# Latent tiles of a PEER layer: gathered expert rows replaced by an ordered walk over the expert table

## What is computed

```
qf = (xt @ w_q)                                # 8 heads x 2 parts of 128
s = einsum('thpd,hpnd->thpn', qf, sub_keys)    # scores of 128 keys per part
sv, si = top_k(s, 16)
cand = sv[:,:,0,:,None] + sv[:,:,1,None,:]     # 256 sums per head
top_s, pos = top_k(cand, 16)
idx = si[0]*128 + si[1] at pos                 # expert number
gate = softmax(top_s)
act = gelu(einsum('td,thkd->thk', x, u_tab[idx]))
out = einsum('thk,thkd->td', gate * act, v_tab[idx])
```

## Time and profile before

| | |
|---|---|
| time, median of 3 runs | 4426.65 us (4425.79 to 4427.81) |
| span of the profiled execution | 4415.7 us, first to last instruction |
| PE, DVE, ACT, POOL busy | 77%, 65%, 20%, 34% |
| PE weight loads busy | 35% |
| DMA | 1494.71 MB, 1344.36 MB of it gathered |
| last stage, from the first product of L777 | 1750 us to the end |

### The profile page before, as it was taken

How to read it: one execution, slowest core, us unless ns; L and a number is a source line. 1 busy time by engine, 2 the same in 40 slices (tenths; PEclk the granted TensorE clock), 3 DMA queues, 4 the chain that set the end, 5 groups by cost and what they waited for, 6 DMA issues and landing times.

```text
span 4415.7 us, 33544 instructions
## 1 busy us (share of the span) xinstructions
PE 3419.6 (77%) x7972; PEld 1528.7 (35%) x7972; DVE 2883.5 (65%) x6259; ACT 887.3 (20%) x2429; POOL 1498.4 (34%) x1297
## 2 busy tenths in 40 slices
PE   7767799976788886777787777777777677777777
PEld 1536344333443443233232333332333233333332
DVE  0535897847556877775775775774775774775774
ACT  0131321454322112111111111111111111111111
POOL 0000222212222223444454354344344444444343
PEclk9878899987898988889988899899899989898899
DMA  6324666756677788999999999999999999999997
GB/s 232 121 85 155 221 231 220 283 197 218 228 282 284 288 325 322 421 421 421 421 421 421 420 414 421 408 409 420 412 406 421 412 404 420 404 411 421 414 408 293
DMA packets 223619, 1494.71 MB, mean 338 GB/s; under 512 B 25388, under 2 KB 26668, under 8 KB 56660
## 3 DMA queue, kind: packets, MB, share of 16 engines
q0 software_dynamic: 184752, 1344.36, 75.7%
q1 hardware_dynamic: 37256, 143.43, 8.7%
q10 hardware_dynamic: 1440, 5.24, 0.3%
HBM read 1466.93 MB, written 26.02 MB: 338 GB/s over the span
## 4 chain that ended last, share of the span: by engine, by line
DMA 46%; PE 26%; DVE 10%; issue 9%; POOL 4%; ACT 3%; SPq 1%; POOLq 0%; DVEq 0%; ACTq 0%; PEldq 0%
DMA arena<-in_uv,idx 29%; DMA ring_e<-in_uv,idx 13%; PE wide L777 5%; PE bank L754 4%; PE bank L597 4%; PE bank L620 3%; PE wide L557 3%; POOL arena L516 3%; PE bank L737 3%; DMA arena<-in_w_q 2%; DVE ring_e L1253 2%; PE bank L568 1%; POOL ring_e L516 1%; PE bank L647 1%; DMA arena<-in_w_mod 1%
## 5 line engine op out<-in xcount | busy, mean ns | idle before, releaser
L777 PE MATMUL wide<-arena 128*128 128x512 f32 x3072 | 1521.6, 653 | 486.2 <-ACT arena L1032 464.0
L1564 DVE CUSTOM_DVE_ANT_0 arena<-arena,h2e 128x1024 f32<-128x1024 f32 x768 | 927.1, 1224 | 535.9 <-DMA arena<-in_uv,idx 511.8
L516 POOL DMA_INDIRECT arena<-in_uv,idx x768 | 900.7, 1173 | 1081.1 <-PE wide L777 918.9
L777 PEld LDWEIGHTS wide<-arena 128*128 128x128 f32 x3072 | 626.0, 209 | 1378.5 <-issue 767.7
L501 POOL DMA_INDIRECT ring_e<-in_uv,idx x256 | 306.0, 1195 | 1076.4 <-PE wide L557 516.3
L777 PE MATMUL wide<-ring_e,arena 128*128 128x512 f32 x1024 | 510.5, 656 | 162.3 <-ACT arena L1032 162.3
L1032 ACT ACTIVATE arena<-ident,small 128x128 f32<-128x128 f32 x1024 | 327.5, 390 | 623.2 <-DVE small L1571 609.5
L1564 DVE CUSTOM_DVE_ANT_0 ring_e<-ring_e,h2e 128x1024 f32<-128x1024 f32 x256 | 309.0, 1224 | 183.4 <-DMA ring_e<-in_uv,idx 183.0
L1253 DVE CUSTOM_DVE_ANT_0 ring_e<-ring_e,h2e 128x1024 f32<-128x1024 f32 x256 | 307.6, 1221 | 171.8 <-DMA ring_e<-in_uv,idx 171.2
L516 POOL DMA_INDIRECT ring_e<-in_uv,idx x256 | 287.0, 1121 | 375.5 <-PE wide L777 326.0
L777 PEld LDWEIGHTS wide<-ring_e,arena 128*128 128x128 f32 x1024 | 209.2, 210 | 463.4 <-issue 248.3
(11 more groups left out here) (180 smaller groups left out, 2413.6 us busy)
## 6 DMA issues: line engine op xcount, KB each, us to landing
arena<-in_w_mod SPq DMA_DIRECT2D x12, 2048.0 KB, 7.8
arena<-in_w_q SPq DMA_DIRECT2D x48, 512.0 KB, 10.4
arena<-in_w_cols SPq DMA_DIRECT2D x24, 512.0 KB, 3.9
arena<-in_uv,idx POOLq DMA_INDIRECT x768
arena<-in_x SPq DMA_DIRECT2D x20, 512.0 KB, 3.7
sc_d<-arena SPq DMA_DIRECT2D x36, 256.0 KB
arena<-in_w_vg SPq DMA_DIRECT2D x16, 512.0 KB, 4.2
arena<-in_w_out SPq DMA_DIRECT2D x16, 512.0 KB, 5.6
```

What stands on the lines that cost most here:

```text
L516: pool.indirect_dma_start(out=ring[k % RING], out_offset=None, in_=a["uv"], in_offset=bass.IndirectOffsetOnAxis(ap=idx[p][:, k:k + 1], axis=0)
L777: ins = pe.matmul(wide[p][:, c * 512:(c + 1) * 512], lhsT=diag[r], rhs=ring[r][:, D + c * 512:D + (c + 1) * 512], start=(first and r == 0) ...
L1564: dve.tensor_tensor_reduce(out=ring[r][:, 0:D], in0=ring[r][:, 0:D], in1=h2b[p], scale=1.0, scalar=0.0, op0=ALU.mult, op1=ALU.add, accum_o ...
```

## The change

Context tiles stay as they are. The latent tiles are taken in three passes of 2, 3 and 3 tiles, and each pass walks through all 128 blocks of 128 experts in order. A step of a pass: SP loads the block's u rows transposed (`in_ut`, a new input laid out by the host, 512 KB) and its v rows (512 KB); `scores_of` makes 8 products with the pass's tokens as columns (256 or 384); ACT takes the gelu from PSUM; `weigh` on DVE multiplies with the dense gates of that block; `sum_rows`, two steps later, adds v with 2 products of 512 columns for each tile.

The dense gates are made once per tile. `turn_choice` transposes the key numbers and gates; for each token DVE makes a one-hot row with the gate in it (`ones_for`), ACT one for the other key (Abs and then Relu over four tokens; of tile 3 DVE makes every second group), `spread` multiplies both into a 128x128 matrix per token, ACT copies four of them (`empty_spread`), SP stores 16 tokens at a time (1 MB, `store_group`) and loads them back for 8 expert blocks at a time (`load_gates`).

The query blocks of the latents become three, tiles 2 and 3, 4 to 6, 7 to 9 (`peer_blocks`), so w_q is loaded once more. Block 3 also holds tile 2's `spread` and tile 3's `pick_step`; tile 3's `spread` stands between it and the first step. Picks of tiles 4 to 7 stand in pass 0, of 8 and 9 in pass 1 (`PICKS`), and `spread` of a pass's tiles in the pass before. The final rows of the context tiles move into block 3; those of a pass stand in the first steps of the next.

```diff
+ETILES = 128
+PASSES = ((2, 2), (4, 3), (7, 3))
+LAG = 2
+UNIT = 4
+NG = 8
+def peer_blocks(s):
+    return [(0, 0, 2)] if s == 0 else [(1 + p, t, n) for p, (t, n) in enumerate(PASSES)]
@@ tensor, query blocks
+                    if b == 3:
+                        turn_choice(2)
                     for hp in range(HP + 1):
                         if hp < HP:
                             ... 8 products of the query
                         if hp:
                             ... scores of hp - 1
+                        if b == 3 and hp < HP:
+                            spread(2, 2 * hp)
+                            spread(2, 2 * hp + 1)
-            with pe.Fori(0, NT // 2 - 1) as i:
-                ... add_rows
+            for t, u in g_tiles[UNITS:2 * UNITS]:
+                if u == 0:
+                    turn_choice(t)
+                spread(t, u)
+            def scores_of(p, i):
+                n, slot = PASSES[p][1], nth[p, i] % URING
+                pe.wait_ge(*ut_in[slot].at((p, i)))
+                bk = claim(s_bank(p, i), S["s_empty"].at((p, i)))
+                for k in range(KD):
+                    ins = pe.matmul(bk[:, 0:n * P], lhsT=utb[slot][:, k * P:(k + 1) * P], rhs=H2T[1 + p][:, k, :], ...)
+            def sum_rows(p, i):
+                pe.wait_ge(*vt_in[slot].at((p, i)))
+                pe.wait_ge(*S["w_ready"].at((p, i)))
+                for j in range(n):
+                    for h, acc in enumerate(acc_banks(j)):
+                        ins = pe.matmul(acc, lhsT=w[:, j * P:(j + 1) * P], rhs=vtb[slot][:, h * 512:(h + 1) * 512], ...)
+            for n, (p, i) in enumerate(sweep):
+                scores_of(p, i)
+                if n >= LAG:
+                    sum_rows(*sweep[n - LAG])
+                for t in choice_in(p + 1, i):
+                    turn_choice(t, claim(g_bank(t, 1), S["sel_ready"].at(t)))
+                for t, u in units_in(p + 1, i):
+                    spread(t, u, claim(g_bank(t, u), S["g_empty"].at((t, u))))
+            def spread(t, u, bk=None):
+                pe.wait_ge(*S["ones_a"].at((t, u)))
+                pe.wait_ge(*S["ones_bv" if vector_ones(t, u) else "ones_b"].at((t, u)))
+                for q in range(UNIT):
+                    ins = pe.matmul(bk[:, c], lhsT=ones_b[n % 2][:, c], rhs=ones_a[n % 2][:, c], start=True, stop=True)
@@ vector, query blocks
                     for hp in range(HP):
+                        if b == 3:
+                            ones_for(2, 2 * hp)
+                            ones_for(2, 2 * hp + 1)
                         bk = wait_full(("sc", b, hp))
                         ... copy of the scores
+                        if b == 3:
+                            for q in share(hp, 0, SPAN_3):
+                                pick_step(3, q)
+            def ones_for(t, u):
+                if n >= 2:
+                    dve.wait_ge(*spread_full(*g_tiles[n - 2]))
+                for q in range(UNIT):
+                    ins = dve.tensor_scalar(ones_a[n % 2][:, c], iota128[:], sel[t % 2][:, k:k + 1],
+                                            sel[t % 2][:, P + k:P + k + 1], ALU.is_equal, ALU.mult)
+            def weigh(p, i):
+                dve.wait_ge(*S["s_empty"].at((p, i)))
+                dve.tensor_tensor(wtb[n % WRING][:, 0:N], act_b[n % 2][:, 0:N], g_, ALU.mult)
@@ host
+        "ut": f["peer_u"][0].reshape(ETILES, P, KD, P).transpose(0, 3, 2, 1).reshape(ETILES, P, D),
```

More of the change, by code:

```diff
@@ L173, in build @@
[L173 to L180, removed]
-        finalb = junk
+        modrow = rreg[0:2, 0:6 * D]
@@ L466, in _ @@
+            for r in range(3):
+                t = max(t for t in range(NT) if t % 3 == r)
+                sp.wait_ge(*S[f"y_out{r}"].at(t))
             sp.wait_ge(*S["state_out"].at(0))
@@ L1022, in _ @@
                     early_share(j, b, HP - 1)
-            def unit(i, p, g, part):
-                j, n = part * GROUP, g * (RING // GROUP) + part + 1
-                act.wait_ge(S["dot"].sem, i * (2 * SLOTS) + (p + 1) * SLOTS + g * RING + j + GROUP)
-                act.activation(gel[:, j:j + GROUP], dots[:, j:j + GROUP], ACT.Gelu).then_inc(S["gelu"].sem, 1)
-                act.wait_ge(S["weight"].sem, i * (2 * SLOTS // GROUP) + p * (SLOTS // GROUP) + n)
-                for r in range(j, j + GROUP):
-                    act.activation(diag[r], ident[:], ACT.Copy, scale=wts[:, r:r + 1]).then_inc(S["diag_ready"].sem, 1)
@@ L1076, in _ @@
+            for t in range(NT - PASSES[-1][1], NT):
+                root(t)
+            for t in range(NT - PASSES[-1][1], NT):
+                store(t)
         @block.vector
@@ new lines, in _ @@
+            for u in range(UNITS):
+                ones_for(3, u)
+            for n, (p, i) in enumerate(sweep):
+                weigh(p, i)
+                for j in range(PASSES[p - 1][1] if p else 0):
+                    t = PASSES[p - 1][0] + j
+                    if i == LAG - 1:
+                        gate_sums(t, j)
+                    if i == 3 + 2 * j:
+                        residual(t)
+                    if i == 5 + 2 * j:
+                        normalised(t)
+                for t in choice_in(p + 1, i):
+                    if t == PASSES[p + 1][0]:
+                        ones_for(t, 0)
+                for t, u in units_in(p + 1, i):
+                    k = g_nth[t, u] + 1
+                    if k < len(g_tiles) and tile_pass(g_tiles[k][0]) == p + 1:
+                        ones_for(*g_tiles[k])
+                for q in range(PICK_STEPS):
+                    for t in chosen_in(p, i, q):
+                        pick_step(t, q)
@@ L1585 @@
+            for j in range(PASSES[-1][1]):
+                gate_sums(PASSES[-1][0] + j, j)
+                residual(PASSES[-1][0] + j)
+            for j in range(PASSES[-1][1]):
+                normalised(PASSES[-1][0] + j)
 FINISH = (5, 2, 2, 2, 4)
```

651 lines of the change are left out of this document (416 added, 235 removed).

## The result

The changed kernel takes 5752.9 us (median of 4 runs, 5749.83 to 5763.61) against 4426.48 us of the kernel before (4 runs, 4425.79 to 4427.81). The ratio is 1.3003, with a 95% interval of 1.2978 to 1.3029: it is slower by 1326 us. The forecast was 5795 us, within 5640 to 5980. The profiled execution took 5749.83 us, its span 5748.1 us.

The account below looks back on a forecast made before the run. The last stage was taken as bound by gather transfers, the changed walk by PE's columns. Start of walk's stage 2057 + wait 12 + walk 3692 + pass changes 5 = 5766, tail 18 to span 5784, plus 10.95: 5795 us, range 5640 to 5980.

Parts of the forecast that it names:

- (a): Whole kernel: the main case, PE's columns set the walk and all else is hidden, 5795 us; chance 0.75.
- The price of a product, and the walk: Walk: 32-bit products cost by columns, 0.86 us for 512; 3520 us plus 172 of `spread`, together 3692 us.
- Changes of pass: Between passes: DVE reads accumulators while PE makes the next scores; 5 us for both, bounds 0 and 150.
- The first wait: Walk's start: one store and one load of 1 MB precede the first `weigh`; wait of 12 us, bounds 0 and 28.
- The front: Up to the last context vector sum: DVE sets the latents' query blocks; sum starts at 1725, bounds 1705 and 1745.
- Block 3: New query block: PE and DVE take turns through `spread` and one-hots; 272 us, to 1997, bounds 130 and 310.
- Rival (c): Block 3: its parts overlap, costing 130 us and not 272, total 5650 us; chance 0.09.
- Tile 3's `spread`: Between block 3 and the walk: DVE's one-hots take 58 us, ACT 51 beside it; 60 with the start, to 2057.
- The tail: After the last product: DVE makes gate, residual and final norm of three tiles where it was one; 18 us.
- Rival (b): Walk: it doesn't close, a wait of 1 us in each step costs 384 us, some 6180 us; chance 0.12.
- Rival (d): Walk: products follow at the pace of weight loads, 190 ns; walk 1946 us, whole 4220 us; chance 0.03.
- Rival (e): Whole change: it doesn't do what it says, for instance leaves the walk short; left at no change, chance 0.01.

Follow-up runs that it names:

- one step of slack: The changed kernel with `sum_rows` one step behind the scores instead of two: 5752.93 us, ratio 1.3001.
- the trace with half gathers: The kernel before, its last stage gathering only the v half of each row and dotting the token with that, the dot with `u` left out: 3816.06 us.
- the padded queries: The changed kernel with dead products ahead of the query products, 8 more per group in block 1 and 3 more in block 2: 5773.74 us.

## Why the prediction was right, step by step

The mechanism was that of the forecast (a), and it is shown: fewer PE columns made it faster at once (one of eight products, 16 bits), and doubled transfers left the walk as it was. That the total came within 42 us (0.7%) is in part luck: of the terms below, five were too high and two too low.

- **What bound the kernel before.** Right: half the bytes of each row took most of the wait for rows away.
- **The price of a product, and the walk.** Right to 0.2%: 3702.9 us less the first wait of 4.6 is 3698.3, forecast 3692 and 5 for the changes of pass. The granted clock was 0.98 in the walk's first 70 us and 1.00 after, where PE waited for nothing, and instructions of 384 columns, for which there was no row, cost 5.16 / 16 = 0.323 us, between those of 256 and 512 by columns.
- **Changes of pass.** The trace has no wait at either; the 5 us were not needed there.
- **The first wait.** 4.55 us, forecast 12 within 0 to 28. It is for a table, but the chain is the forecast's: SP's list has the last store, then the wait for it to land, then `load_gates`, then the third step's table.

```profile
2034.29 7.55 DMA arena<-in_ut
```

SP issued the last store at 2030.0 and, once it had landed, the load of gates at 2033.86 and this table at 2034.29. `weigh` waited 13.0 us for its first gates, to 2040.6, while PE had scores to make; with one step of slack the wait of 5.0 is for these weights. So the term was mis-sized, at 12 for 4.55, because both transfers landed soon, the store in 3.8 us and the load in some 6.8. The 512-byte pieces of `load_gates` are cheap: 1 MB lands in 7.7 us and 1.5 MB in 9.6 (medians of 16 and 32 loads), beside the tables, and from 2034 to 2046 the rate is 318 GB/s at a DMA share of 0.94. The rule of the Trainium skill ("DMA: Bandwidth & Descriptors", Specifications: 512 B as the least size at full rate) fits that. Its fit, which the page gives for transfers that GpSimd issues and not for SP's, made 4.4 us of the 1 MB, less than the 7.7 here; its answer, no wait for gates, was nearer than my term.
- **The front.** The term outside its bounds. The last vector sum starts at 1687.9; forecast was 1725, within 1705 to 1745. Part of the place is chance: block 1 begins at 1395.9 here, and between 1384.5 and 1405.3 in the other kernels with the same front, at 1407.9 before. But from there to the last sum it took 328.8 us before (337.7 in the trace with half gathers) and 291.0 to 292.9 in eight traces with the changed front. My term was 12 of these 37. The step that failed is "the query blocks of the latents are set by DVE": PE's columns are two fifths to a half of it, as the padded queries show. In windows of the two blocks DVE has 8.6 us less work as well; 6.4 us of this are the copies of the scores (21.9 us before, 15.5 now).

Before, blocks 1 and 2, and the same of the changed kernel (columns as above, DVE's busy time is the third):

```profile
1408.00:1555.00 147.00, 130.35 (x384) 65.22 (x385) 111.77 (x233) 17.73 (x58) 35.80 (x28) 0.95 0.75 275
1574.00:1737.00 163.00, 133.44 (x384) 66.37 (x384) 122.78 (x198) 24.30 (x67) 40.28 (x32) 0.92 0.82 313
```

```profile
1396.00:1522.00 126.00, 79.88 (x321) 66.07 (x322) 102.91 (x231) 14.08 (x58) 34.99 (x28) 0.80 0.85 319
1540.00:1688.00 148.00, 108.23 (x372) 67.48 (x372) 123.04 (x201) 20.58 (x67) 36.30 (x29) 0.85 0.74 274
```

PE was at 130 of 147 us and DVE at 112: neither had room to be late for the other. I read DVE's sum and took PE as covered, with 7.8 us of work in a turn of 9.2. That DVE's 8.6 us carry the rest is argued from these windows, not shown; it stays open.

- **Block 3.** Right: from the last vector sum to the turn to tile 3 it took 265.8 us (1687.9 to 1953.7), forecast 272. From the first `spread` group to the sixteenth (1700.5 to 1942.6) a turn takes 16.1 us on average, forecast near 16. PE waits for DVE's one-hots behind the copy and the picks in the second half, as [10.27 <-DVE] in the rows above says; in five of the first nine turns it is ACT's Relu that comes last, with 5.1 us each. Moving DVE's one-hots ahead gave 36.5 us. Rival (c), 130 us, was not near; even with the better order it is 305.8 with tile 3 for 342.3, for the next chain, ACT's, lies right below.
- **Tile 3's `spread`.** 76.5 us (1953.7 to 2030.2), forecast 60. The mis-sized term is ACT, and a wait for a store stood in no term. Two groups take 4.01 us, of which ACT is busy for all but 0.33: two copies of 1.03, four Abs in 1.24, a Relu of 0.63, together 3.93 with some overlap. The copy `empty_spread` was put at 0.6 by the contiguous copy of 128x512; it writes with a stride and takes 1.04 us on average:

```profile
L1068 ACT ACTIVATE arena<-bank 128x512 f32<-128x512 f32 x256 | 265.0, 1036 | 876.1 <-PE bank L720 868.7 <-DMA spread_d<-arena 7.0 <-ACT sel L1042 0.4
```

  Where DVE was named as the limit with 58 us, ACT has 63. The 7.0 us in this row are one wait, to 1964.1: tile 3's first copy needs the buffer of a group of tile 2 whose store hasn't landed. SP issued it at 1953.7 only, for in its list it stands behind the last scores and the walk's first four tables. From the first of the 16 pairs of groups to the last it is 69.6 us: 15 x 4.01 = 60.2, 5.7 more in the turn with that wait, and 3.7 in four turns of 4.92, whose products took 3.7 us and not 2.0. The start adds 3.6 us and the end 3.3. The other traces with this front have the wait at 6.3 to 10.0 us, and at 16.1 with doubled loads.
- **The tail.** 15.0 us from the last product, forecast 18.
- **Around the span.** I added 10.95 us, the difference between the median and the profiled span of before. It is 1.73 (5749.83 less 5748.1), and 1.7 in the kernel before too, when both are given for one run (4423.33 and 4421.6). So some 9 of the 10.95 were no overhead, and the profiled execution of before must have been that much faster than the median.

The sum closes: front -37, block 3 -6, tile 3 +16.5, first wait -7.5, walk +1.3, tail -3 make -36, from 5784 to 5748 of span; 9 less around it, and the median is 3 above the profiled run: 5753. Of the signs, "transfers at 150 to 190 GB/s" held in pass 0 alone (189); passes 1 and 2 have 135 and 123.

Rival (b) found nothing to hold it: neither one step of slack nor doubled loads opens the walk. Rival (d) is refuted by the pace in the rows above: 0.429 us at 512 columns, also in a stream of 3698 us. The 131 ns that the Trainium skill ("TensorE: Matmul & The Clock Gate", Back-to-back issue gap) gives for such a stream appears neither here nor in 16 bits, where 0.215 us stands, near the page's isolated gap of 216 ns; the measurement decides. Rival (e) is refuted too: the trace has all 10240 instructions of the walk.

## What to carry to other kernels

Before bytes are traded for dense products, price the products by columns and width of type from a dense stretch, and ask how much air the bound engine has above the next one: here half the bytes gave 607 us, all of them could give some 900 by estimate, and the products cost 3698 where 2666 stood. The same walk's products in 16 bits cost a quarter on PE, and so the trade that loses 30% in 32 bits wins 18% with it, and 19% with the better order in block 3. A part that two engines take in turns is as long as its chain: put first in an engine's list what the other one waits for (in SP's list too, where a store stood behind tables that were not due yet), and count both engines' work when both are as busy as in the query blocks before (PE 130 and DVE 112 of 147 us).

## What the runs showed of the hardware that was not expected

- Transfers that convert 32 to 16 bits fill the DMA engines (share 1.05) at 204 GB/s written, about 344 GB/s read by the estimate above. Plain 32-bit table loads had 322 GB/s at 0.93, so halving the bytes written didn't make the tables cheaper. Gathers of 32-bit rows reached 419 GB/s at 1.01.
- ACT's copy of 128x512 from PSUM took 586 ns contiguous and 1036 ns with strided output.
- The same 16 instructions of `spread` took 3.78 us after an idle time of 10.27 us (1888.36 above), at a granted clock of 0.50, the level of 1.2 GHz, and 2.02 us after one of 1.99 (1975.91), at 1.00. From 1700 to 2000, with block 3 and the start of tile 3, the granted clock was 0.79; the walk had 0.98 in its first 70 us and 1.00 after.
